# Split-weight offsets by kind of unit, regrouped low products, and two block boundaries taken one token tile at a time

## The chip, the cores and the metric

The kernel runs on one core of a Trainium2 chip. The metric is device microseconds (us) of one launch; lower is better. TensorE (PE) does the matrix products, its weight loads are listed as PEld, VectorE is DVE, ScalarE is ACT, GpSimd is POOL, and SP issues the weight stream.

## The reference, cut to what matters

Three transformer layers on x (256 tokens x 1024, fp32). Layer 1: differential attention beside a causal pool, cross-attention to a memory of 256 tokens, a SwiGLU of width 2816, each with a norm before and a norm after. Layer 2: retention beside sparse attention, then SwiGLU. Layer 3: HGRN2, then SwiGLU, then the final norm. What the change touches:

```python
x = x + rmsnorm(attn @ w_xo, g_x_post)          # "xo"
hf = rmsnorm(x, g_ffn_pre)
ff = (silu(hf @ w_gate) * (hf @ w_up)) @ w_down # "gu0", "dn0"
x = x + rmsnorm(ff, g_ffn_post)
proj = rmsnorm_2(x, norm_mix_g[0]) @ even_w_in  # "ev", first units: the queries
```

## The kernel before, in words

**Units.** All weights come as a stream of 165 units of 128 x 2048 fp32 (1 MB). SP loads unit u into `raw[:, u % 4]`; ACT writes its rounded high part to `whi` (`split`, L453); DVE writes the rest, raw minus high, to `wlo` (L937); PE uses both. PE waits for `lo_ready`, ACT for `unit_done` of the unit four back, SP for `lo_ready` of the unit four back. Activations are split as well: `x2[:, kt, :]` holds for block kt of 128 channels 256 columns of high parts (`xTh`) and then 256 of low parts (`xTl`); `hTh`/`hTl` hold the hidden layer.

**Kinds of unit.** Each product is high*high + high*low + low*high.
- *columns* (22 units on x, 4 on the memory): weights stationary, activations moving, 48 matmuls of 256 columns (`passes`, L1732 to L1734).
- *rows* (14 on x, 4 on the memory): activations stationary, weights moving, 48 of 256.
- *sums* ("out", "xo", "eo", "oo" and the three "dn"): activations stationary, weights moving, 24 of 512: four PSUM banks, two blocks, three passes (`sum_unit`). "xo" and "out" take `x2`, and so do half of "eo" and "oo"; the other halves take `nh` and `ah`; the 33 "dn" units take `hTh`/`hTl`.
- *gate/up* (66 units, `wide_columns`): per kt two matmuls of 512 columns (high weights on all of `x2[:, kt]`, L1770) and two of 256 (low weights on `xTh`, L1768, for kt 0 L1774).

**SBUF offsets.** From the widths of the allocations: `raw`, `whi` and `wlo` start alike modulo 512 bytes, and a ring slot is 8192 bytes; pads put `x2` 64 bytes further modulo 512, `hTh`/`hTl` 256 bytes further, `memTh`/`memTl` 32. While PE streams the moving operand of one matmul, the weights of the next are read. The table has the moving operand's address minus the weights' address, modulo 256 bytes, before and after the change (a slot becomes 8448 bytes, so modulo 512 the difference alternates with the slot's parity after it).

| kind of unit | before | after |
|---|---|---|
| columns on x / on the memory | 64 / 32 | 192 / 192 |
| rows on x / on the memory | 192 / 224 | 192 / 192 |
| gate/up, 512 columns / 256 columns | 64 / 64 | 0 / 192 |
| sums from x2 / nh / ah | 192 / 64 / 0 | 0 / 0 / 0 |
| sums from hTh | 0 | 0 (low weights of the first two "dn" units: 64) |

**Boundary "xo" to gate/up (n=3).** `sum_unit` finishes unit after unit; only the last unit completes the four banks, one after another (bank c is chunk c: tokens 0 to 127 are chunks 0 and 1). `post_norm` then goes per chunk: ACT squares (L522), DVE `gained` (L1023), mean, POOL power (L375), DVE `update` (L1030), which counts up `x_part`. PE's `boundary` transposes chunk 0, runs two dummy fp32 matmuls (`keep_clock`, L1821), then chunk 2, chunk 1, low products, chunk 3; ACT (`norm_hi`, L471) and DVE (`norm_lo`, L965) split the transposed blocks in eight steps of 256 columns. `first_wide` is unit gu0+0; behind it `rb_spread` (L1988) transposes the row scales, on which ACT waits (`rb_copy`) before it splits unit gu0+3, and DVE behind it:

```python
def norm(n, last, first):            # ACT
    ...
    split(last - 1 + RING)
    rb_copy(n)
    split(last + RING)
```

The boundary from "dn0" to "ev" (n=4) is the same with `first_columns`.

**Gate/up loop.** For each pair of units DVE does, in this order: reduce gate (L1072), times rb (L1082), `split` of unit +4, reduce up (L1072), times gate (L1091), `split` of unit +5, low part of h (L1096). ACT's silu (L537) waits on L1082, and its splits of units +4 and +5 stand behind the silu. Before the first "dn" unit PE also waits for `up_sum` of pair 9 (the first L1072 of `s_hb` behind the split of dn0+0).

Of the kernel before, what the change touches and what calls it, by code (L numbers as in the profile page):

```python
# [37 lines left out]
UNIT = 2048  # L38
RING = 4
# [36 lines left out]

POW_N = {"subln": 8, "gn0": 4, "gn1": 4, "hg0": 8, "hg1": 8}
# [27 lines left out]
N_GAIN = _at  # L105

# [13 lines left out]
def build(nc, stream, x_in, mem_in, pos_in, gains_in, rows_in, consts_in, poolm_in, wpool_in, retm_in,  # L120
# [12 lines left out]
    with ctx:  # L133

        raw = sb(ctx, "raw", [P, RING, UNIT])
        whi = sb(ctx, "whi", [P, RING, UNIT], F32R)
        wlo = sb(ctx, "wlo", [P, RING, UNIT], F32R)
# [6 lines left out]
        gains = sb(ctx, "gains", [P, N_GAIN])  # L144
# [14 lines left out]
        def gain(name, k=0):  # L159
# [8 lines left out]
        a_ = ExitStack()  # L168
        memTh = sb(a_, "memTh", [P, KT, S], F32R)
# [15 lines left out]
        posi = sb(a2, "posi", [P, S], I32)  # L185
        a2.close()
# [8 lines left out]
        sb(f_, "h_pad", [P, 56])  # L195
# [37 lines left out]
        sb(b4, "nh_pad", [P, 8])  # L233
# [9 lines left out]
        kd = sb(c_, "kd", [P, 8, S])  # L243
# [7 lines left out]
        sb(c_, "ah_pad", [P, 56])  # L251
        ah = sb(c_, "ah", [P, 4, S], F32R)
        al = sb(c_, "al", [P, 4, S], F32R)
        oh = qd[:].rearrange("p (g t a) (b n) -> p g t (a b) n", g=2, t=NT, n=P)
# [14 lines left out]
                 ("ffn1", "f1", 6)]  # L269

# [29 lines left out]
        def norm_banks(n):  # L300

            if n == 2:
                return [DB[2], DB[3], TB[0], TB[1]]
            ph = {3: "xo", 4: "dn0", 5: "eo", 6: "dn1", 7: "oo"}.get(n)
            return DB if ph is None else [b for k, b in banks.items() if k not in SUMS[ph]]
# [63 lines left out]
        def _(pool):  # L369
# [18 lines left out]
            pool.dma_start(gains[:, GAIN["lam"][0]:], gains_in[:, GAIN["lam"][0]:]).then_inc(sem("lam_in"), 16)  # L388
# [53 lines left out]
        def _(act):  # L442
            def split(u, i=None):
# [9 lines left out]
                nc.scalar.activation(whi[:, u % RING, 0:n], raw[:, u % RING, 0:n], ACT.Copy)\  # L453
                    .then_inc(hi_ready, 1)

            def norm_squares(n, src, scratch, version=None, parts=range(4)):

                for c in parts:
# [3 lines left out]
                    if n == 0 and c % 2 == 0:  # L462
                        act.wait_ge(sem(f"x_in{c // 2}"), 16)
                    nc.scalar.activation(scratch(c), chunk(src, c), ACT.Square, scale=D ** -0.5,
                                         accum_out=ss[:, 16 + c:17 + c]).then_inc(sem("norm_sq"), 1)

# [12 lines left out]
            def norm(n, last, first):  # L479
                norm_squares(n, xn, lambda c: chunk(y, c), NORMS[n][2], range(first))  # L480
                norm_hi(n, xTh)
# [32 lines left out]
            def post_squares(ph):  # L514

                for c in range(4):
                    wait_sum(act, ph, c)
# [38 lines left out]
            act.dma_start(gains[:, 0:GAIN["lam"][0]], gains_in[:, 0:GAIN["lam"][0]]).then_inc(sem("gains_in"), 16)  # L556
# [165 lines left out]
            post_squares("xo")  # L722
# [4 lines left out]
            post_squares("dn0")  # L727
# [192 lines left out]
        def _(dve):  # L920
# [8 lines left out]
            def split(u, i=None):  # L929

                if u >= N_UNITS:
# [5 lines left out]
                nc.vector.tensor_tensor(wlo[:, u % RING, 0:n], raw[:, u % RING, 0:n],  # L937
                                        whi[:, u % RING, 0:n], ALU.subtract).then_inc(lo_ready, 1)
# [20 lines left out]

            def norm_lo(n, dst_h, dst_l, kts=range(KT)):  # L960
# [14 lines left out]
            def norm_rest(n, last, between=None):  # L975

                name = NORMS[n][1]
                norm_lo(n, xTh, xTl)
# [8 lines left out]
            def evac_scaled(u, dst, src=None):  # L987
# [4 lines left out]
                    .then_inc(bank_read[bank(u)], 1)  # L992

# [16 lines left out]
            def post_norm(k0, ph, name):  # L1010
# [28 lines left out]
                gained(2)  # L1039
                update(1)  # L1040
# [127 lines left out]
            lam = gains[:, GAIN["lam"][0]:GAIN["lam"][0] + 256]  # L1168
# [154 lines left out]
            post_norm(1, "xo", "p_x")  # L1323
# [5 lines left out]
            post_norm(2, "dn0", "p_ffn")  # L1329
# [4 lines left out]
            def first_queries():  # L1334
                dve.wait_ge(sem("rb_ready"), 2)
                evac_scaled(u0, nqT[:, 0:2, :], DB[0])

            norm_rest(4, BASE["dn0"] + DN - 1, first_queries)
            evac_scaled(u0 + 1, nqT[:, 2:4, :])
# [388 lines left out]
        def _(pe):  # L1728
# [17 lines left out]
            def columns(u, act_h, act_l, ready=None):  # L1746

                hi = whi[:, u % RING, :].rearrange("p (k n) -> p k n", k=KT)
                lo = wlo[:, u % RING, :].rearrange("p (k n) -> p k n", k=KT)
# [10 lines left out]
            def wide_columns(u, o):  # L1760

                hi = whi[:, u % RING, :].rearrange("p (k n) -> p k n", k=KT)
                lo = wlo[:, u % RING, :].rearrange("p (k n) -> p k n", k=KT)
                c = [slice(P * f, P * f + P) for f in range(2)]
                for kt in range(KT):
                    if kt >= 1:
                        for f in range(2):
                            nc.tensor.matmul(o[:, f, 0:S], lo[:, kt, c[f]], xTh[:, kt, :], start=False, stop=False)  # L1768
                    for f in range(2):
                        ins = nc.tensor.matmul(o[:, f, :], hi[:, kt, c[f]], x2[:, kt, :], start=kt == 0,  # L1770
                                               stop=kt == KT - 1)
                    if kt == 0:
                        for f in range(2):
                            nc.tensor.matmul(o[:, f, 0:S], lo[:, kt, c[f]], xTh[:, kt, :], start=False, stop=False)  # L1774
                return ins

            def values_and_gates(u):

                n, c = 256 + NG_COLS, UNIT * (u % RING)
# [11 lines left out]
            def rows(u, act_h, act_l, ready=None, o=None, between=None):  # L1791

                hi = whi[:, u % RING, :].rearrange("p (k n) -> p k n", k=KT)
                lo = wlo[:, u % RING, :].rearrange("p (k n) -> p k n", k=KT)
# [23 lines left out]
            def keep_clock(bank_, times):  # L1818

                for _ in range(times):  # L1820
                    nc.tensor.matmul(bank_[:], ident, same_rows(cst[:, 0:256], 2), start=True, stop=True)  # L1821

# [11 lines left out]
            def first_unit():  # L1834

                hi, lo = (w[:, 0, :].rearrange("p (k n) -> p k n", k=KT) for w in (whi, wlo))
# [813 lines left out]
```

## Time and profile before

| | |
|---|---|
| median of 3 runs | 1045.02 us (1044.1 to 1045.32) |
| profiled execution | 1042.93 us, its span 1040.8 us |
| PE busy / weight loads | 1027.2 us (99%) / 914.5 us (88%) |
| DVE / ACT / POOL busy | 736.6 / 520.6 / 31.7 us |
| granted TensorE clock | 0.999 of 2.4 GHz |

Matmuls are pipelined, so a matmul's own duration (0.28 us for 256 columns, 0.39 for 512) says little; the time from one start to the next is what PE takes for it. "Busy 99%" means only that PE was rarely without work in flight.

### The profile page before, as it was taken

Reading aid. Unit: us, or ns where it says so; the run is one execution under the profiler, and the core shown is the slowest. Engines: PE = TensorE matmul, PEld = TensorE weight load, DVE = VectorE, ACT = ScalarE, POOL = GpSimd, SP = SyncE. Lnnn points to the kernel's source line nnn. Section 1 sums busy time; section 2 is a strip of 40 time slices with the busy share of each in tenths; the row PEclk is TensorE's granted clock in tenths of the full one; section 3 lists DMA queues with packets and bytes.
Section 4 is the critical chain, followed back from the end, with each engine's and each line's share of the span. In section 5 each row is a group of like instructions: output and inputs, shape, how many; then the busy total and the mean of one; then the engine's idle time right before and its main releaser. Section 6 shows DMA issues by size and latency. Waiting matters only on the chain.

```text
span 1040.8 us, 17117 instructions
## 1 busy us (share of the span) xinstructions
PE 1027.2 (99%) x6908; PEld 914.5 (88%) x6908; DVE 736.6 (71%) x946; ACT 520.6 (50%) x673; POOL 31.7 (3%) x49
## 2 busy tenths in 40 slices
PE   8999999999999999999999999999999999999997
PEld 7998898788888889999888888889999988888885
DVE  6987564568878545898768788646788767778842
ACT  6875474454344435865453443435543354443531
POOL 1000100000000001000000000001000100000000
PEclk9999999999999999999999999999999999999999
DMA  9834463255554746444235545655444235545531
GB/s 346 342 128 149 169 223 122 81 183 176 192 197 164 276 167 264 165 145 139 93 127 191 196 164 199 245 200 187 161 160 147 98 122 204 200 161 197 191 137 41
DMA packets 27292, 183.41 MB, mean 176 GB/s; under 512 B 3200, under 2 KB 3472, under 8 KB 6112
## 3 DMA queue, kind: packets, MB, share of 16 engines
q1 hardware_dynamic: 25056, 175.01, 47.2%
q0 software_dynamic: 1744, 7.16, 1.9%
q8 instruction: 46, 0.75, 0.3%
q10 hardware_dynamic: 432, 0.37, 0.1%
q14 instruction: 14, 0.11, 0.0%
HBM read 181.48 MB, written 1.05 MB: 175 GB/s over the span
## 4 chain that ended last, share of the span: by engine, by line
PE 94%; DVE 3%; ACT 2%; issue 1%; POOL 0%; DVEq 0%; ACTq 0%
PE GT L1770 12%; PE D L1770 11%; PE GT L1732 9%; PE GT L1734 9%; PE GT L1733 9%; PE D L1733 7%; PE D L1732 7%; PE D L1734 7%; PE GT L1768 5%; PE D L1768 5%; PE D L2443 1%; PE GT L1945 1%; DVE s_wlo L937 1%; PE GT L1774 1%; PE D L1774 1%
## 5 line engine op out<-in xcount | busy, mean ns | idle before, releaser
L937 DVE TENSOR_TENSOR s_wlo<-s_raw,s_whi 128x2048 fp32r<-128x2048 f32 x164 | 372.8, 2277 | 176.7 <-ACT s_whi L453 176.2
L453 ACT ACTIVATE s_whi<-s_raw 128x2048 fp32r<-128x2048 f32 x164 | 307.6, 1900 | 91.9 <-PE D L1734 68.7
L1770 PE MATMUL GT<-s_x,s_whi 128*128 128x512 f32 x528 | 162.1, 393 | 0.0
L1770 PE MATMUL D<-s_x,s_whi 128*128 128x512 f32 x480 | 146.9, 392 | 0.0
L1732 PE MATMUL D<-s_whi,s_hTh 128*128 128x512 f32 x264 | 102.9, 390 | 0.0
L1733 PE MATMUL D<-s_wlo,s_hTh 128*128 128x512 f32 x264 | 102.7, 389 | 0.0
L1734 PE MATMUL D<-s_whi,s_hTl 128*128 128x512 f32 x264 | 102.7, 389 | 0.0
L1732 PE MATMUL GT<-s_x,s_whi 128*128 128x256 f32 x352 | 99.6, 283 | 0.0
L1768 PEld LDWEIGHTS GT<-s_x,s_wlo 128*128 128x128 f32 x462 | 84.4, 188 | 16.9
L1734 PE MATMUL GT<-s_x,s_wlo 128*128 128x256 f32 x352 | 98.3, 279 | 0.0
L1733 PE MATMUL GT<-s_x,s_whi 128*128 128x256 f32 x352 | 98.2, 279 | 0.0
L1768 PE MATMUL GT<-s_x,s_wlo 128*128 128x256 f32 x462 | 91.4, 279 | 0.0
L1732 PE MATMUL GT<-s_whi,s_x 128*128 128x256 f32 (+2 forms) x296 | 90.9, 307 | 0.0
L1768 PEld LDWEIGHTS D<-s_x,s_wlo 128*128 128x128 f32 x420 | 76.8, 188 | 15.4
L1734 PE MATMUL GT<-s_whi,s_x 128*128 128x256 f32 (+2 forms) x296 | 89.0, 301 | 0.0
L1733 PE MATMUL GT<-s_wlo,s_x 128*128 128x256 f32 (+2 forms) x296 | 89.0, 301 | 0.0
L537 ACT ACTIVATE s_sg<-s_sg 128x512 f32<-128x512 f32 x33 | 20.9, 632 | 128.2 <-DVE s_sg L1082 128.2
L1770 PEld LDWEIGHTS GT<-s_x,s_whi 128*128 128x128 f32 x528 | 82.3, 188 | 2.5
L1768 PE MATMUL D<-s_x,s_wlo 128*128 128x256 f32 x420 | 83.1, 279 | 0.0
L1770 PEld LDWEIGHTS D<-s_x,s_whi 128*128 128x128 f32 x480 | 75.0, 188 | 2.5
L1732 PEld LDWEIGHTS GT<-s_x,s_whi 128*128 128x128 f32 x352 | 66.0, 187 | 0.3
L1733 PEld LDWEIGHTS GT<-s_x,s_whi 128*128 128x128 f32 x352 | 66.1, 188 | 0.0
(385 smaller groups left out, 1735.2 us busy)
## 6 DMA issues: line engine op xcount, KB each, us to landing
s_raw<-in_stream SPq DMA_DIRECT2D x164, 1024.0 KB, 4.8
s_gb<-in_rows POOLq DMA_DIRECT2D x4, 512.0 KB, 4.2
s_xn<-in_x SPq DMA_DIRECT2D x2, 512.0 KB, 4.3
s_raw<-in_stream SPq DMA_DIRECT2D x4, 256.0 KB, 6.6
s_y<-in_mem POOLq DMA_DIRECT2D x1, 1024.0 KB, 10.1
s_w<-in_cmpw POOLq DMA_DIRECT2D x1, 1024.0 KB, 11.5
s_poolm<-in_poolm POOLq DMA_DIRECT2D x1, 768.0 KB, 11.7
s_retd<-in_retm POOLq DMA_DIRECT2D x1, 768.0 KB, 7.1
```

What stands on the lines that cost most here:

```text
L453: nc.scalar.activation(whi[:, u % RING, 0:n], raw[:, u % RING, 0:n], ACT.Copy)\
L537: nc.scalar.activation(sg[:, q % 2, :], sg[:, q % 2, :], ACT.Silu).then_inc(sem("silu_made"), 1)
L937: nc.vector.tensor_tensor(wlo[:, u % RING, 0:n], raw[:, u % RING, 0:n], whi[:, u % RING, 0:n], ALU.subtract).then_inc(lo_ready, 1)
L1732: nc.tensor.matmul(out_, sh, mh, start=start, stop=False)
L1733: nc.tensor.matmul(out_, sh, ml, start=False, stop=False)
L1734: return nc.tensor.matmul(out_, sl, mh, start=False, stop=stop)
L1768: nc.tensor.matmul(o[:, f, 0:S], lo[:, kt, c[f]], xTh[:, kt, :], start=False, stop=False)
L1770: ins = nc.tensor.matmul(o[:, f, :], hi[:, kt, c[f]], x2[:, kt, :], start=kt == 0, stop=kt == KT - 1)
L1774: nc.tensor.matmul(o[:, f, 0:S], lo[:, kt, c[f]], xTh[:, kt, :], start=False, stop=False)
L1945: ins = nc.tensor.matmul(o[:, f, :], hi[:, kt, c], x2[:, kt, :], start=False, stop=kt == KT - 1)
L2443: ins = nc.tensor.matmul(DB[2 * hg + idx % 2][half * part:half * part + half, c:c + w], kd[:, h, tk], queries, start=True, stop=True)
```

## The change

1. `whi` and `wlo` slots get a pitch of 2112 elements, and `places(u)` shifts each unit's high and low part in its slot by 0, 16, 32 or 64 elements by its kind. Pads move `memTh`, `hTh`, `nh`, `ah` to match; `lam` gets its own tile; `ah` shares memory with `kd`.
2. `wide_columns` does all 16 low matmuls together, behind the first two high ones.
3. `last_sums`: the last two units of "xo" and "dn0" are summed bank by bank (12 matmuls each), and chunks 0 and 1 are transposed inside the fourth bank.
4. `first_pair` replaces `first_wide` of gu0 and `first_columns` of "ev": units 0 and 1 together, first the high weights on token tile 0, then the transposes of chunks 2 and 3, then tile 1 and all low products: 48 matmuls of 256 columns per unit. `tile_hi`/`tile_lo` split the transposed blocks in 8 steps of 128 columns for each tile. `rb_spread` follows the pair. `keep_clock` is gone.
5. `evac_wide` (a reduction and a product on DVE) takes the place of `evac_scaled` for ev+0 and ev+1.

```diff
+PITCH = UNIT + 64
+ROWS, SUM, COLUMNS, JOINED = 0, 16, 32, 64
+def places(u):
+    name = max((b, name) for name, b in BASE.items() if b <= u)[1]
+    j = u - BASE[name]
+    if name.startswith("gu") or name in ("ev", "dn0", "dn1", "dn2") and j < 2:
+        return SUM, COLUMNS
+    if name in SUMS or name == "out2":
+        return SUM, SUM
...
@@ ACT
+            def tile_hi(n, t):
+                for kt in range(KT):
+                    if kt % 4 == 0:
+                        if t == 0:
+                            act.wait_ge(sem("first_tr"), 2 * (n - 3) + kt // 4 + 1)
+                        else:
+                            act.wait_ge(sem("norm_tr"), 4 * n + kt // 2 + 2)
...
             def post_squares(ph, n=None):
                 for c in range(4):
+                    if n is not None and c == 3:
+                        tile_hi(n, 0)
@@ DVE post_norm
+                    update(1)
+                    gained(2)
+                    tile_lo(n, 0)
                 dve.wait_ge(sem("post_sq"), 4 * k0 + 4)
@@ PE wide_columns
+                for f in range(2):
+                    nc.tensor.matmul(o[:, f, :], hi[:, 0, c[f]], x2[:, 0, :], start=True, stop=False)
                 for kt in range(KT):
-                    if kt >= 1:
-                        for f in range(2):
-                            nc.tensor.matmul(o[:, f, 0:S], lo[:, kt, c[f]], xTh[:, kt, :], start=False, stop=False)
                     for f in range(2):
+                        nc.tensor.matmul(o[:, f, 0:S], lo[:, kt, c[f]], xTh[:, kt, :], start=False, stop=False)
+                for kt in range(1, KT):
+                    for f in range(2):
+                        ins = nc.tensor.matmul(o[:, f, :], hi[:, kt, c[f]], x2[:, kt, :], start=False,
@@ PE
+            def last_sums(ph, n, read, ready):
+                last = N_OF[ph] - 1
...
+                for b, o in enumerate(sum_banks(ph)):
...
+                    for j in (last - 1, last):
...
+                        for kk in range(2):
+                            if b == 3 and j < last and kk == 1:
+                                chunk_transposes(n, 0)
+                                chunk_transposes(n, 1)
...
+            def first_pair(n, u, pair):
...
+                for k, o in enumerate(pair):
+                    wait_unit(u + k)
+                    for kt in range(KT):
+                        pe.wait_ge(sem("first_tile_lo"), KT * (n - 3) + kt + 1)
+                        high_weights(u + k, o, 0, kt, start=kt == 0, stop=False)
+                chunk_transposes(n, 2)
+                chunk_transposes(n, 3)
+                for k, o in enumerate(pair):
+                    lo = low(u + k).rearrange("p (k n) -> p k n", k=KT)
+                    for kt in range(KT):
+                        pe.wait_ge(sem("xT_ready"), KT * n + kt + 1)
+                        high_weights(u + k, o, 1, kt, start=False, stop=False)
...
@@ PE mlp
+                        if i is None and q == 0 and f == 0:
+                            if c == 0:
+                                first_pair(n, u, gate_up_banks(0))
+                                rb_spread(n)
+                            continue
```

## Rows read from the trace of the kernel before

**Rows 1.** The page, parts 1 and 2: busy time, granted clock by slice.
```profile
PE 1027.2 (99%) x6908; PEld 914.5 (88%) x6908; DVE 736.6 (71%) x946; ACT 520.6 (50%) x673; POOL 31.7 (3%) x49
...
PEclk9999999999999999999999999999999999999999
```

**Rows 2.** Timeline, PE: "xo" and "dn0" sums. Start us, length us, instruction.
```profile
192.21 0.39 PE L1732 MATMUL GT<-s_whi,s_x 128*128 128x512 f32 x1
...
201.78 0.40 PE L1734 MATMUL D<-s_whi,s_x 128*128 128x512 f32 x1
...
378.94 0.39 PE L1732 MATMUL D<-s_whi,s_hTh 128*128 128x512 f32 x1
...
388.23 0.39 PE L1734 MATMUL D<-s_whi,s_hTl 128*128 128x512 f32 x1
```

**Rows 3.** Timeline, PE: gate/up units of gu0.
```profile
218.12 0.40 PE L1774 MATMUL D<-s_x,s_wlo 128*128 128x256 f32 x2
...
287.00 0.40 PE L1768 MATMUL D<-s_x,s_wlo 128*128 128x256 f32 x2
287.23 0.62 PE L1770 MATMUL D<-s_x,s_whi 128*128 128x512 f32 x2
...
323.49 0.40 PE L1774 MATMUL GT<-s_x,s_wlo 128*128 128x256 f32 x2
```

**Rows 4.** Timeline, PE: memory rows, slow and fast rows, columns on x.
```profile
91.36 0.28 PE L1733 MATMUL GT<-s_wlo,s_memTh 128*128 128x256 f32 x1
...
96.81 0.28 PE L1734 MATMUL GT<-s_whi,s_memTl 128*128 128x256 f32 x1
...
477.70 0.28 PE L1733 MATMUL GT<-s_wlo,s_x 128*128 128x256 f32 x1
...
483.12 0.28 PE L1734 MATMUL GT<-s_whi,s_x 128*128 128x256 f32 x1
...
717.86 0.28 PE L1733 MATMUL GT<-s_x,s_whi 128*128 128x256 f32 x1
...
727.17 0.28 PE L1734 MATMUL GT<-s_x,s_wlo 128*128 128x256 f32 x1
...
776.36 0.28 PE L1733 MATMUL GT<-s_wlo,s_x 128*128 128x256 f32 x1
...
781.58 0.28 PE L1734 MATMUL GT<-s_whi,s_x 128*128 128x256 f32 x1
```

**Rows 5.** Timeline, all engines: the boundaries behind "xo" and behind "dn0".
```profile
201.05 0.75 DVE L1030 SCALAR_TENSOR_TENSOR s_xn<-s_y,s_rstd,s_xn 128x512 f32<-128x512 f32 x1 [0.15 <-POOL s_rstd L375]
...
202.45 1.88 PE L1821 MATMUL GT<-s_cst 128*128 128x512 f32 x4
...
203.86 1.41 DVE L1030 SCALAR_TENSOR_TENSOR s_xn<-s_y,s_rstd,s_xn 128x512 f32<-128x512 f32 x2
...
206.80 1.57 ACT L471 ACTIVATE s_x<-GT,s_gains 128x256 fp32r<-128x256 f32 x4
...
207.68 1.66 DVE L965 SCALAR_TENSOR_TENSOR s_x<-GT,s_gains,s_x 128x256 fp32r<-128x256 f32 x4
...
211.87 0.38 PE L1988 MATMUL D<-s_cst,s_rstd 128*128 128x128 f32 x2
...
398.49 0.38 PE L1988 MATMUL D<-s_cst,s_rstd 128*128 128x128 f32 x2
```

**Rows 6.** Timeline, DVE and PE: the vector chain of gu0, its first and last pairs.
```profile
216.79 1.22 DVE L1072 TENSOR_REDUCE s_sg<-GT 128x512 f32<-128x1024 f32 x1
...
221.31 2.29 DVE L937 TENSOR_TENSOR s_wlo<-s_raw,s_whi 128x2048 fp32r<-128x2048 f32 x1 [2.50 <-ACT s_whi L453]
...
232.62 2.29 DVE L937 TENSOR_TENSOR s_wlo<-s_raw,s_whi 128x2048 fp32r<-128x2048 f32 x1 [2.50 <-ACT s_whi L453]
...
325.41 1.22 DVE L1072 TENSOR_REDUCE s_hb<-D 128x512 f32<-128x1024 f32 x1
...
328.59 0.39 PE L1732 MATMUL D<-s_whi,s_hTh 128*128 128x512 f32 x1
```

More of the change, by code:

```diff
@@ L74 @@
 LATE_KV = ("kv5", "out2", "kv6")
+ROWS, SUM, COLUMNS, JOINED = 0, 16, 32, 64
[6 more added lines that the diff above has]
+        return SUM, SUM
+    if name == "ev" and j == 4:
+        return JOINED, JOINED
+    columns = {"in": (4, 5, 6, 7), "kv": (0, 1, 2, 3), "xq": (0, 1, 2, 3), "ev": (0, 1, 2, 3, 6, 7, 8, 9),
+               "od": range(8)}
+    return (COLUMNS, COLUMNS) if j in columns.get(name, ()) else (ROWS, ROWS)
 POW_N = {"subln": 8, "gn0": 4, "gn1": 4, "hg0": 8, "hg1": 8}
@@ L105 @@
 N_GAIN = _at
+LAM = GAIN["lam"][0]
 def bank_reads(u):
@@ L269, in build, with high, low @@
                  ("ffn1", "f1", 6)]
+        def high(u, n=UNIT):
+            return whi[:, u % RING, places(u)[0]:places(u)[0] + n]
+        def low(u, n=UNIT):
+            return wlo[:, u % RING, places(u)[1]:places(u)[1] + n]
         def halves(ap):
@@ L452, in split @@
                 n = KT * NG_COLS if u == NG_UNIT else UNIT
-                nc.scalar.activation(whi[:, u % RING, 0:n], raw[:, u % RING, 0:n], ACT.Copy)\
+                nc.scalar.activation(high(u, n), raw[:, u % RING, 0:n], ACT.Copy)\
                     .then_inc(hi_ready, 1)
@@ L977, in norm_rest @@
                 name = NORMS[n][1]
-                norm_lo(n, xTh, xTl)
+                if n < 5:
+                    tile_lo(n, 1)
+                else:
+                    norm_lo(n, xTh, xTl)
                 norm_mean(n, name, 0)
@@ L1038, in post_norm @@
                 update(0)
-                gained(2)
-                update(1)
+                if n is None:
+                    gained(2)
+                    update(1)
+                else:
+                    update(1)
+                    gained(2)
+                    tile_lo(n, 0)
                 dve.wait_ge(sem("post_sq"), 4 * k0 + 4)
@@ L1834, in first_unit @@
             def first_unit():
-                hi, lo = (w[:, 0, :].rearrange("p (k n) -> p k n", k=KT) for w in (whi, wlo))
+                hi, lo = (w(0).rearrange("p (k n) -> p k n", k=KT) for w in (high, low))
                 def step(t, kt, stat, mov, start=False, stop=False):
@@ L1864, in second_unit @@
             def second_unit(u):
-                hi, lo = (w[:, u % RING, :].rearrange("p (k n) -> p k n", k=KT) for w in (whi, wlo))
+                hi, lo = (w(u).rearrange("p (k n) -> p k n", k=KT) for w in (high, low))
                 o = G[bank(u)]
@@ L1927, in first_wide, with part @@
             def first_wide(u, o, n):
-                def low(f):
+                def part(f):
                     return o[:, f, 0:S]
-                hi = whi[:, u % RING, :].rearrange("p (k n) -> p k n", k=KT)
-                boundary(n, u, low, 1)
+                hi = high(u).rearrange("p (k n) -> p k n", k=KT)
+                boundary(n, u, part, 1)
                 for kt in range(KT):
@@ L1937, in first_wide @@
                     if kt >= 4:
-                        block_low(u, low, n, kt, 1)
+                        block_low(u, part, n, kt, 1)
                     for f in range(2):
@@ L1970, in first_queries @@
                 u, n = BASE["xq"], 2
-                hi, lo = (w[:, u % RING, :].rearrange("p (k n) -> p k n", k=KT) for w in (whi, wlo))
+                hi, lo = (w(u).rearrange("p (k n) -> p k n", k=KT) for w in (high, low))
                 wait_unit(u)
@@ L2052, in mlp @@
                 pe.wait_ge(sem("up_sum"), p0 + GU // 2 - 1)
-                for d in range(DN):
+                for d in range(DN - 2 if f == 0 else DN):
                     pe.wait_ge(sem("h_lo"), p0 + d + 1)
                     sum_unit(f"dn{f}", d, hTh, hTl, n=6 if f == 1 and d == DN - 1 else None)
+                if f == 0:
+                    last_sums("dn0", 4, "h_lo", p0)
             pe.wait_ge(sem("warm_in"), 1)
@@ L2237, in _ @@
             x_out(3)
-            for j in range(1, 4):
-                pe.wait_ge(sem("x_lo"), j + 1)
-                sum_unit("xo", j)
+            pe.wait_ge(sem("x_lo"), 2)
+            sum_unit("xo", 1)
+            last_sums("xo", 3, "x_lo", 0)
             mlp(0)
@@ L2264, in ret_out @@
                     .then_inc(sem("ret_out"), 1)
-            first_columns(u0, 4)
+            first_pair(4, u0, (DD[:, 0:2, :], GT[:, 2:4, :]))
             rb_spread(4)
-            for j in range(1, 4):
+            for j in range(2, 4):
                 unit(u0 + j, columns)
```

142 lines of the change are left out of this document (95 added, 47 removed).

## The prediction

> **What bounds the kernel now.** The page comes first. PE is busy 99% of the span at a granted clock of 0.999, which is its upper level of 2.4 GHz, and DVE 71% [rows 1]. So the time is that of PE's matmuls one after another, and a change can only shorten it by making PE start them closer together, by taking out waits of PE, or lengthen it by making PE wait. The second view is PE's timeline, read from start to start. In "xo" 42 matmuls of 512 columns start over 9.57 us, 233.4 ns each; in "dn0" 42 of the same form over 9.29 us, 226.6 ns each [rows 2]. Clock, size and pattern are the same; what differs is the difference of the two operands' addresses (192 against 0 in the table of offsets). A gate/up unit takes (323.49 - 218.12) / 19 = 5.546 us; a pair of its low products takes 0.23 us, so that each of the 16 of 512 columns takes about 230 ns [rows 3]. Units of 256-column matmuls have two paces. Columns on x: 9.31 us over 79 steps, 117.8 ns (21 of the 22 units). Rows on x: 5.22 / 46 = 113.5 ns in ten units, 5.42 / 46 = 117.8 in four, with the same offsets. Memory rows: 118.5 [rows 4]. The third view is the timeline of all engines at the two boundaries, where PE waits for the post norm; the fourth is DVE's in gate/up, which shows how far the supply of low parts is ahead of PE.
>
> **Offsets.** I take the address difference as the cause of the paces, since it is what the two groups of [rows 2] do not share.
> - Sums from x2, without xo+2 and xo+3: 240 matmuls x 6.8 ns = -1.6 us. For those from nh and ah I take nothing; the bound is -0.6.
> - Gate/up, 512 columns: difference 0, so 226.6. Its 256-column ones get the difference of the row units on x, whose mean is (10 x 113.5 + 4 x 117.8) / 14 = 114.7. A unit: 16 x 226.6 + 16 x 114.7 = 5.461 us, 0.085 less. 42 units of gu1 and gu2: -3.6 us. Regrouping the low products adds nothing: the counts are the same, and low behind low and low behind high take alike.
> - Columns on x, without ev+1: 21 x 48 = 1008 matmuls, 117.8 to 114.7, -3.1 us. Bounds: -4.3 (all fast) and 0 (all slow).
> - Memory, 384 matmuls at 118.5 or 117.8: -1.3 us, between -1.8 and 0.
> - The low weights of two units in each "dn" have difference 64: 48 matmuls at 230 for 226.6, +0.15 us.
>
> The Trainium skill, TensorE: Matmul & The Clock Gate, section "Step-by-step: what each phase is for", speaks against all of this: PE reads moving operand and weights through two independent ports, and loading the next weights takes no bandwidth from the running matmul. By that rule offsets are worth nothing. The 233.4 beside 226.6 does not agree with it; it is the fourth rival below.
>
> **Boundary behind "dn0".** Before, from the start of the second-last unit: 48 x 226.6 = 10.88 us to 388.46, then 10.03 to the row scales at 398.49 [rows 5], 0.2 for them, and ev+1 in 48 x 117.8 = 5.65: 26.8 us until ev+2 can start. After: 10.88; eight transposes inside it, 0.88 (four took 202.01 to 202.45); 32 high matmuls on tile 0 at 115 ns, 3.68; eight transposes, 0.88; a wait; 64 matmuls, 7.36; 0.2.
>
> Are tile 0's parts there in time? Count from the end of bank 1. Before, that was 12 matmuls ahead of the end of bank 3 at 202.01, or 199.21, and the first `update` began 1.84 us behind it, at 201.05, the second follows 0.7 later, so chunk 1 is ready at 3.5; PE reaches its transposes at 2.72 + 0.68 + 0.44 = 3.84. ACT takes 1.57 for four blocks of 256 columns and DVE 1.66 [rows 5]. A block of 128 costs half to all of that; I take two thirds, 0.26, nearer to half because the fixed part of an instruction stays. Then tile 0 is split by 7.6, and PE, which gets there at 6.3, takes 0.23 per kt and stays behind the supply. Bank 3's square, mean, power and updates end near 9.9; PE wants chunks 2 and 3 at 10.0 and 10.4. All that hides. What does not: tile 1's first four highs, then its first low, behind the transposes of chunk 2: 0.2 + 4 x 0.27 + 0.1 + 0.4 - 0.44 (chunk 3) = 1.4 us of wait, where before 2.2 us went to waiting and dummy matmuls (202.45 to 204.67). Bounds of the wait: 0.9 and 2.0. After: 10.88 + 0.88 + 3.68 + 0.88 + 1.4 + 7.36 + 0.2 = 25.3. That is -1.5 us. `evac_wide` (a reduction of 1.2 us and a product) comes between DVE's splits of ev+2 and ev+3, which have 5.5 us of PE work as cover: nothing, and up to 2 us if the cover failed.
>
> **Boundary behind "xo" and all of gu0.** The same step costs here, because it moves `rb_spread` behind two units. ACT's `rb_copy` and its split of gu0+3 wait for it, DVE's split of gu0+3 waits for ACT, and behind that stands the first gate reduction, with which the chain of the phase starts. Call the time of the row scales F. Before F is 211.87, the first reduction starts at 216.79, and the low part of gu0+4 is done at 221.31 + 2.29 = 223.60 = F + 11.7. The chain's period is 232.62 - 221.31 = 11.31 us, longer than PE's pair of 11.09, and it was ahead because PE still had gu0+1 to do behind F. Now PE has only gu0+2 and gu0+3: it wants gu0+4 at F + 0.2 + 2 x 5.46 = F + 11.1. So it waits 0.6 us, and then 11.31 - 10.92 = 0.4 us in each pair: gu0 runs at DVE's pace, whatever its offsets give. The "dn" start waits for `up_sum` of pair 9, at 326.63 = F + 114.8 [rows 6], and dn0+2 starts 10.9 later. From the start of xo+2 (190.81) to dn0+2 (328.59 + 10.88 = 339.47), before: 148.7 us. After: 10.88 (now at 226.6) + 0.88 + 3.68 + 0.88 + 1.4 + 7.36 + 125.7 = 150.8. +2.1 us. In gu1 and gu2 nothing is moved; PE gets there 21 x 0.085 = 1.8 us earlier and the margin is 328.59 - 326.63 = 1.96, so they just escape, and a larger gain than 2 us in either would be lost.
>
> **Sum.** -1.6 - 3.6 - 3.1 - 1.3 + 0.15 - 1.5 + 2.1 = -8.9 us. Of the units in the attention phases some end in front of a wait for another engine, which takes back part; I allow 0.4. -8.5 us against the profiled execution's 1042.9 gives 1034.4 us. That execution is 2.1 us below the median of the runs, so for the median 1045.0 - 8.5 = **1036.5 us**.
>
> **Rivals.**
> 1. *DVE's chain does not bind gu0.* It would have to be ahead at F by 5.3 us more than I reckon; for it speaks only that my F rests on the boundary's reckoned wait. gu0 then gives 20 units at 5.461: 145.4 for 150.8, 1031 us.
> 2. *The 256-column matmuls stay at 117.8.* For it: the row units show both paces at the same offsets, and one column unit was fast at the old ones, so the offset is not all. Then columns and memory give 0.1, gate/up 16 x 3.4 - 16 x 0.8 = 0.04 per unit, 1.7 us, and the rest stays: about -2.5, 1042.5 us.
> 3. *Slower.* No 512-column matmul of the kernel before has a difference of 0 modulo 512 bytes: "dn0" stands at 256 or 768. The new slot pitch gives half of the units 0. If those run at 226.6 + x, the price is (396 of "dn" + 192 of other sums + 336 of gu1 and gu2) = 924 matmuls times x. Against it: the slowest pace seen is 233.4. From x = 9 ns (236) the gain is gone, from 11.5 (238) the kernel is slower by over 0.2%; at 240 it takes about 1049 us.
> 4. *Offsets do nothing.* Then only the boundaries count: +2.5 and -1.3, 1046.2 us.
>
> **How the numbers follow.** The forecast 0.5, with 1034 to 1039 as its own range; rival 1 0.14; rival 2 0.17; rival 3 0.07; rival 4 0.07; something else 0.05. The range from rival 1 to rival 2 and its edge, 1031 to 1043, leaves out rivals 3 and 4 and part of the rest. A measurement of this kernel tells about 0.2% (2.1 us) from no change. Faster by more than that: the forecast, rival 1, two thirds of rival 2, part of the rest, 0.79. Within it: the remainder of rival 2, rival 4 and the mild form of 3, 0.12. Slower 0.09.
>
> **What the profile after would show.** "xo" and "out" sums at 226.6 ns per start; gate/up units of gu1 at 5.46 us; column units below 117.8; slots of both parities alike (rival 3 if not). At the boundaries one PE wait near 1.4 us, on DVE's first low part of tile 1, and no L1821. In gu0 a PE wait of 0.4 us on DVE's low part in every second unit, a period of 11.3 us per pair, and none in gu1 and gu2. The prediction is wrong if gu0 shows no such waits, or if the paces do not follow the table of offsets.

## The result, and the profile after

The changed kernel takes 1045.43 us in the median of 20 runs (1042.56 to 1047.22), the kernel before 1043.44 beside it (20 runs, 1042.68 to 1045.56): a ratio of 1.0016, 95% interval 1.0009 to 1.0022. It is slower by about 1.7 us (the medians differ by 2.0), where 8.5 us less were forecast. The profiled execution took 1046.54 us, 3.6 more than that of before; it is the third slowest of its 20 runs.

The page of the changed kernel, parts 1 and 4, and its waits of PE from 214 to 500 us (two views, the second from 340; us in total, times, longest):

```profile
span 1044.4 us, 17188 instructions
...
PE 1025.2 (98%) x6930; PEld 915.7 (88%) x6930; DVE 741.3 (71%) x964; ACT 523.7 (50%) x689; POOL 31.5 (3%) x49
...
PE 80%; DVE 8%; ACT 6%; issue 6%; DVEq 0%; ACTq 0%
...
PE D L1814 <- DVE s_hb L1155: 1.2, 1, 1.2
PE GT L1848 <- DVE s_wlo L991: 0.4, 1, 0.4
...
PE GT L1814 <- DVE s_nqT L1070: 2.6, 1, 2.6
PE D L2015 <- DVE s_x L1024: 1.2, 1, 1.2
```

PE's busy time did fall by 2.0 us against [rows 1], but the chain of work that ended last now runs through DVE and ACT for 14% of the span. On the page of the kernel before that line reads:

```profile
PE 94%; DVE 3%; ACT 2%; issue 1%; POOL 0%; DVEq 0%; ACTq 0%
```

That is a share of the chain and not time lost: most of it is DVE's chain in gu0, which PE now follows. The largest single wait of PE, 2.6 us for the evacuation of ev+0, is not in the prediction's sum.

PE's timeline after, at the points that answer to [rows 2 to 6] (start, length, instruction, idle before it):

```profile
189.35 0.39 PE L1814 MATMUL GT<-s_whi,s_x 128*128 128x512 f32 x1
...
207.19 0.51 PE L2015 MATMUL GT<-s_x,s_whi 128*128 128x256 f32 x2 [1.18 <-DVE s_x L1024]
...
226.72 0.72 PE L1848 MATMUL GT<-s_x,s_whi 128*128 128x512 f32 x2 [0.39 <-DVE s_wlo L991]
...
237.97 0.73 PE L1848 MATMUL D<-s_x,s_whi 128*128 128x512 f32 x2
...
249.37 0.72 PE L1848 MATMUL GT<-s_x,s_whi 128*128 128x512 f32 x2
...
329.74 0.47 PE L1814 MATMUL D<-s_whi,s_hTh 128*128 128x512 f32 x1 [1.20 <-DVE s_hb L1155]
...
340.96 0.39 PE L1814 MATMUL D<-s_whi,s_hTh 128*128 128x512 f32 x1
...
379.06 0.39 PE L1814 MATMUL D<-s_whi,s_hTh 128*128 128x512 f32 x1
...
407.49 0.36 PE L1814 MATMUL GT<-s_x,s_whi 128*128 128x256 f32 x1 [2.55 <-DVE s_nqT L1070]
...
549.11 0.61 PE L1848 MATMUL D<-s_x,s_whi 128*128 128x512 f32 x2
549.56 2.05 PE L1851 MATMUL D<-s_x,s_wlo 128*128 128x256 f32 x16
551.45 3.36 PE L1854 MATMUL D<-s_x,s_whi 128*128 128x512 f32 x14
554.65 0.61 PE L1848 MATMUL GT<-s_x,s_whi 128*128 128x512 f32 x2
...
727.78 0.28 PE L1814 MATMUL GT<-s_x,s_whi 128*128 128x256 f32 x1
...
733.22 0.28 PE L1814 MATMUL GT<-s_x,s_whi 128*128 128x256 f32 x1
```

In gu0 the units at 226.72, 237.97 and 249.37 are every second one. They start 11.25 and 11.40 us apart, where two units without a wait take 11.08: PE waits a little in each pair, mostly too briefly to be listed as a wait. A gate/up unit outside gu0 takes 554.65 - 549.11 = 5.54 us, as before (5.546): its 16 low products start 118 ns apart (551.45 - 549.56), and its 14 high ones behind them take 3.20 us, 228.6 each. The column unit from 727.78 takes 5.44 us over 48 starts, 113.3. And the windows view, which shows what the wait at 407.49 brought with it (columns: PE busy, granted clock, DMA share, GB/s):

```profile
404.40:407.40 3.00, 0.54 (x5) 1.00 1.03 407
407.40:411.60 4.20, 4.11 (x22) 0.60 0.99 392
411.60:438.00 26.40, 25.96 (x272) 1.00 0.65 241
438.00:442.50 4.50, 4.50 (x38) 0.62 0.49 204
```

Behind the wait the granted clock is at its lower level, 1.2 GHz, for 3.3 us (from 408.2 to 411.5 it is 0.51), and it is there again for some 3 us from 439. A column matmul then starts 213 ns behind the last one and not 113 to 118; 16 and 14 such starts make 1.5 and 1.4 us. Before, the clock was 1.00 all the way from 390 to 440.

Every run has a mean granted clock on record, and the time goes with it. Of the changed kernel's 20 runs 13 are at 0.996 or less; of the 81 runs of the kernel before beside the experiments one is. The four runs of the changed kernel at 0.998 have a mean of 1043.7 us (1042.56 to 1045.37), the seven at 0.995 one of 1046.1; the 48 of before at 0.998 have 1043.0. So most of the loss in the median comes with the lower clock. This compares few runs, on chips that are partly not the same, and is not an experiment.

Where the 3.6 us of the two profiled executions come from, by PE's starts (ends of the stretches as in [rows 2 to 5] and above):

| stretch | before | after | difference |
|---|---|---|---|
| to the start of xo+2's sums | 190.81 | 189.35 | -1.5 |
| xo+2 to dn0+2 (boundary, gu0) | 148.7 | 151.6 | +2.9 |
| second-last dn0 unit to ev+2 | 26.8 | 28.4 | +1.6 |
| ev+2 to the first "eo" sum (both half-clock stretches) | 96.9 | 99.9 | +3.0 |
| the rest | | | -2.4 |

### The profile page after: what moved, and what is told of

Read it like the earlier page. It is cut to its first block, busy times and chain, and to the rows that moved or that the text cites. A ratio compares the mean times of both kernels' runs of the same rounds, so it can differ in the third digit from the quotient of the medians.

```text
span 1044.4 us, 17188 instructions
## 1 busy us (share of the span) xinstructions
PE 1025.2 (98%) x6930; PEld 915.7 (88%) x6930; DVE 741.3 (71%) x964; ACT 523.7 (50%) x689; POOL 31.5 (3%) x49
## 4 chain that ended last, share of the span: by engine, by line
PE 80%; DVE 8%; ACT 6%; issue 6%; DVEq 0%; ACTq 0%
PE GT L1814 8%; PE GT L1815 8%; PE GT L1816 8%; PE D L1814 7%; PE D L1816 7%; PE D L1815 7%; PE GT L1854 7%; PE D L1854 6%; PE GT L1851 4%; PE D L1851 4%; ACT s_whi L489 3%; DVE s_wlo L991 2%; PE D L2577 1%; DVE s_hb L1155 1%; PE GT L2015 1%
## 5 line engine op out<-in xcount | busy, mean ns | idle before, releaser
L1854 PE MATMUL GT<-s_x,s_whi 128*128 128x512 f32 x448 | 107.6, 391 | 0.0
L1854 PE MATMUL D<-s_x,s_whi 128*128 128x512 f32 x420 | 100.9, 391 | 0.0
L1814 PE MATMUL GT<-s_x,s_whi 128*128 128x256 f32 x336 | 96.4, 287 | 2.6 <-DVE s_nqT L1070 2.6
L1854 PEld LDWEIGHTS GT<-s_x,s_whi 128*128 128x128 f32 x448 | 82.0, 188 | 15.7
L1815 PE MATMUL GT<-s_x,s_whi 128*128 128x256 f32 x336 | 94.9, 283 | 0.0
L1816 PE MATMUL GT<-s_x,s_wlo 128*128 128x256 f32 x336 | 94.9, 282 | 0.0
L1814 PEld LDWEIGHTS GT<-s_x,s_whi 128*128 128x128 f32 x336 | 64.8, 193 | 3.0 <-issue 2.8
L1851 PEld LDWEIGHTS GT<-s_x,s_wlo 128*128 128x128 f32 x512 | 64.7, 189 | 2.5
L1851 PE MATMUL GT<-s_x,s_wlo 128*128 128x256 f32 x512 | 65.4, 281 | 0.0
L1816 PEld LDWEIGHTS GT<-s_x,s_wlo 128*128 128x128 f32 x336 | 64.8, 193 | 0.0
L1815 PEld LDWEIGHTS GT<-s_x,s_whi 128*128 128x128 f32 x336 | 64.7, 193 | 0.0
L1851 PEld LDWEIGHTS D<-s_x,s_wlo 128*128 128x128 f32 x480 | 60.6, 189 | 2.3
```

Of the source, the lines that this page charges most:

```text
L1814: nc.tensor.matmul(out_, sh, mh, start=start, stop=False)
L1815: nc.tensor.matmul(out_, sh, ml, start=False, stop=False)
L1816: return nc.tensor.matmul(out_, sl, mh, start=False, stop=stop)
```

## The experiments

All ratios are against the kernel before on the same chip, with 95% intervals.

**The parts by themselves.** Three kernels divide the change: its offsets alone, its boundaries alone, and offsets with the grouped low products.

```diff
 # e1: offsets; old boundaries, old order        # e2: old offsets and order; new boundaries
-PITCH = UNIT                                    -    first_wide(...); first_columns(u0, 4)
+PITCH = UNIT + 64                               +    last_sums(...); first_pair(...)
+... high(u), low(u) with places(u)              # e5: e1 and the low products of gate/up together
```

> The changed kernel's offsets and pads, with the order of the kernel before: its post-norm boundaries and its low products between the high ones in gate/up. Theory A (the offsets pay, the new boundaries lose it): sums from x2 near 227 to 229 ns, the two first units of each dn near 232, no wait in gu0; about 3 us below the kernel before, 1040.5. Rival B (the offsets do nothing or cost): within 1 us of the kernel before, 1043.4.

> The changed kernel's boundaries (chunkwise last sums, first pair tile by tile) on the layout, offsets and gate/up order of the kernel before. Theory A: 2.6 us lost from the end of xo to dn0, 1.6 us at the boundary behind dn0, and 1.6 to 2.9 us more because PE's granted clock falls behind its wait there: 1048.5 to 1050. Rival B (the loss belongs to the offsets): within 2 us of the kernel before.

> The changed kernel with both post-norm boundaries of the kernel before: offsets and low products together, nothing else. Theory A (in gate/up the new offsets alone cost 0.054 us per unit, 5.600 for 5.546, and taking the low products together gives 0.060): 63 units times 0.060 below the kernel with the offsets alone, 1044.2 - 3.8 = 1040.4 us, units of 5.54. Rival B (the units keep 5.60 without the boundaries' order around them): 1044.

| kernel | us | ratio |
|---|---|---|
| e1, offsets | 1044.18 | 1.0012 (1.0003 to 1.0021) |
| e2, boundaries | 1048.54 | 1.0050 (1.0038 to 1.0063) |
| e5, offsets and grouping | 1040.68 | 0.9968 (0.9955 to 0.9981) |

The boundaries alone cost 0.5%; offsets and grouping together gain 0.32%. The boundaries came out as expected of e2, and e5 as its theory A. But e1 missed its expectation: offsets alone, with the old interleaved order, gain nothing (rival B). PE's timeline of e1, the first low product (kt 0) of two gate/up units in a row:

```profile
543.25 0.40 PE L1858 MATMUL D<-s_x,s_wlo 128*128 128x256 f32 x2
...
548.85 0.40 PE L1858 MATMUL GT<-s_x,s_wlo 128*128 128x256 f32 x2
```

5.60 us, where [rows 3] give 5.546: the new offsets cost gate/up 0.054 us a unit (512 columns start 233.8 ns apart), 3.4 us over the 63 units that are not the first of their phase. That eats the gain of the sums. The grouping gives 0.06 back: 63 x 0.06 = 3.8, as measured between e1 and e5 (3.5 us, or 4.6 by the ratios).

**Is it the grouping or the offset that helps gate/up?**

```diff
 # e6: offsets of before, grouped     # e7: e5, but in places(u):
-PITCH = UNIT + 64                    -        return SUM, COLUMNS   # gu*, and dn0 to dn2, ev with j < 2
+PITCH = UNIT                         +        return SUM, SUM
```

> The layout and offsets of the kernel before, its boundaries, and only the low products of gate/up together. Theory A (a run of 512-column matmuls goes at 226.6 only at a difference of 0; at 64 it goes at some 232, as the first two units of each dn do): a gate/up unit of 16 x 117.8 + 14 x 232 + 2 x 227 = 5.59 us, 1043.0 + 63 x 0.04 = 1045.5. Rival B (grouping alone sets the unit, offsets do nothing in gate/up): units of 5.54, 1042.6.

> As the kernel with the old boundaries, the new offsets and the low products together, but the low parts of gate/up, of the first two units of each dn and of ev+0 and ev+1 at offset 16 instead of 32. The first two units of each dn then have difference 0: 227 instead of 232 ns per matmul, 6 units x 0.13 = 0.8 us less. For the 256-column matmuls of gate/up: theory A (their pace does not follow the difference) units stay at 5.54, 1039.6 in all; rival B (a difference of 192 is what lets 256 columns go fast) they slow down beyond 117.8; at 119 to 121 it is 63 x 16 x 1.2 to 3.2 ns more, 1040.8 to 1042.8.

e6: 1041.12 us, 0.9977 (0.9967 to 0.9986); e7: 1041.05 us, 0.9978 (0.9967 to 0.9988). PE's timeline of e6, then of e7, from gate/up unit to unit:

```profile
535.85 0.62 PE L1844 MATMUL D<-s_x,s_whi 128*128 128x512 f32 x2
536.31 1.98 PE L1847 MATMUL D<-s_x,s_wlo 128*128 128x256 f32 x16
...
541.32 0.62 PE L1844 MATMUL D<-s_x,s_whi 128*128 128x512 f32 x2
541.78 2.05 PE L1847 MATMUL D<-s_x,s_wlo 128*128 128x256 f32 x16
...
546.88 0.39 PE L1844 MATMUL GT<-s_x,s_whi 128*128 128x512 f32 x1
```

```profile
538.07 0.62 PE L1850 MATMUL D<-s_x,s_whi 128*128 128x512 f32 x2
538.52 2.08 PE L1853 MATMUL D<-s_x,s_wlo 128*128 128x256 f32 x16
...
543.63 0.39 PE L1850 MATMUL D<-s_x,s_whi 128*128 128x512 f32 x1
```

In e6 units take 5.47 and 5.56 us in turn, 5.52 in the mean. Both theories of e6 were wrong: at a difference of 64 the grouped unit is not slower but faster than with the change's offsets (5.54), because every second run of 256-column products goes at 113.3. Its 512-column ones start 229 ns apart in the mean, not 232 as theory A had it. In e7, where the 256-column products stand at a difference of 0, they take 119.6 ns each and a unit 5.56 us; rival B was right for the pace. The first two units of each "dn" went from some 232 to 226.7, as reckoned. The medians of e5, e6 and e7 lie within 0.4 us and do not tell these layouts apart; the starts do. So grouping pays at either layout, and in gate/up the change's offsets take part of it back.

**The wait at ev+2.** ev+0 and ev+1 now stand in D and in banks 2 and 3 of GT; ev+2 and ev+3 write banks 0 and 1 of GT. They waited all the same, since `wait_bank` counts units and not banks. e3 leaves the two units out of the count, e8 does so with the old boundary behind "xo", which is also tried by itself (e4). e4 and e8 have the dummy matmuls behind "xo" again, but not behind "dn0".

```diff
 # e3 and e8
             n = bank_reads(u)[bank(u)]
+            if u in (BASE["ev"] + 2, BASE["ev"] + 3):
+                n -= 1
 # e4 and e8: sum_unit("xo", j) for j in 1..3, first_wide and keep_clock behind "xo"
```

> The changed kernel, but ev+2 and ev+3 no longer count the evacuations of ev+0 and ev+1, whose banks are others. Theory A (that wait of 2.55 us, and the half clock of 3.3 us behind it, are the loss at this boundary): no wait at ev+2, granted clock 1.0 there, 3 to 4 us below the changed kernel, about 1041.5 to 1042.5. Rival B (DVE's chain is only uncovered one step later): ev+3 or ev+4 waits 1 to 2.5 us instead, and less than 1.5 us is gained.

> The changed kernel with the old boundary behind xo (whole units, first unit alone, dummy matmuls), and the new one behind dn0. Theory A (the new step behind xo moves the row scales behind two units and makes gu0 run at DVE's pace): no waits in gu0, dn0 starts 2.6 us earlier against the end of xo, about 1043. Rival B (gu0's waits only take up what the boundary had gained): within 0.5 us of the changed kernel.

> The old boundary behind xo, the new one behind dn0, and ev+2 and ev+3 not counting the evacuations of ev+0 and ev+1. Theory A (the two losses add): what the bank wait cost in the profile, 2.6 us of wait and up to 1.6 of half clock, off the 1042.15 of the kernel with the old boundary behind xo: 1038.5 to 1040.5. Rival B (the new boundary behind dn0 brings a stretch of half clock somewhere in ev anyway, or DVE is late at ev+3): 1041 to 1042.

| kernel | us | ratio |
|---|---|---|
| e3, no bank wait | 1044.08 | 1.0011 (1.0002 to 1.0020) |
| e4, old boundary behind "xo" | 1042.15 | 0.9991 (0.9981 to 1.0002) |
| e8, both | 1040.22 | 0.9965 (0.9953 to 0.9978) |

First the changed kernel at this place, PE, ACT and DVE; then e3:

```profile
404.56 0.38 PE L2115 MATMUL D<-s_cst,s_rstd 128*128 128x128 f32 x2
...
404.98 0.38 ACT L526 ACTIVATE s_rb<-D 128x256 f32<-128x256 f32 x1 [4.47 <-PE D L2115]
...
405.39 1.22 DVE L1069 TENSOR_REDUCE s_nqT<-D 128x512 f32<-128x1024 f32 x1 [2.56 <-ACT s_rb L526]
406.65 0.69 DVE L1070 TENSOR_TENSOR s_nqT<-s_nqT,s_rb 128x512 f32<-128x512 f32 x1
```

```profile
378.46 0.39 PE L1814 MATMUL D<-s_whi,s_hTh 128*128 128x512 f32 x1
...
404.09 0.36 PE L1814 MATMUL GT<-s_x,s_whi 128*128 128x256 f32 x1
...
424.80 0.36 PE L1814 MATMUL GT<-s_x,s_whi 128*128 128x256 f32 x1 [0.99 <-ACT s_vsw L809]
```

and e3 by windows (PE busy, granted clock, DMA share, GB/s):

```profile
421.00:424.80 3.80, 2.81 (x72) 1.00 0.64 203
424.80:428.40 3.60, 3.60 (x18) 0.54 0.87 282
```

Row scales, copy, reduction and product, 2.8 us in a row, used to lie behind ev+1; with both units done at once nothing lies over them. In e3 ev+2 starts at once and the boundary takes 404.09 - 378.46 = 25.6 us (25.3 predicted, 26.8 before). In its profiled execution that is 3.9 us of span less (1040.5 for 1044.4): the wait, and one of the two stretches at half clock. Its median fell by only 1.35 us, and its interval overlaps that of the changed kernel (0.5 us by the ratios), so the medians do not show the gain. The profiled executions exaggerate it: e3's (1042.72) is the fastest of its 11 runs, the changed kernel's is among its slowest. One wait is new in e3: PE gets to ev+6 earlier and waits 0.99 us there for ACT to read out the values of ev+4, and the clock falls at that point. In e8 the same step took 1.9 us off e4's median, 2.7 by the ratios, and e8's granted clock is 1.00 from 400 to 450. Theory A holds for the wait, and rival B for part of its worth in e3; e8 is inside its own theory A.

e4 shows the other boundary by itself: PE waits nowhere from 204 to 345 us, and from the start of xo+2 to that of dn0+0 it takes 137.47 us, where the changed kernel takes 140.39 and the kernel before 137.78. Its theory A holds.

**The waits in gu0.** Two different cures for DVE's chain, each with both new boundaries and without the bank wait: in e9 the next high split comes ahead of the silu, in e10 the split of gu0+3 comes ahead of the copy of the row scales.

```diff
 # e9, ACT, pair(q)                              # e10, ACT, norm(3)
+    split(u0 + 2 * q + RING, i)                      split(last - 1 + RING)
     act.wait_ge(sem("gate_sum"), ...)           -    rb_copy(n)
     nc.scalar.activation(... ACT.Silu)               split(last + RING)
-    split(u0 + 2 * q + RING, i)                 +    rb_copy(n)
```

> Both new boundaries, ev+2 and ev+3 without the bank wait, and in gate/up ScalarE splits the next gate unit ahead of the silu instead of behind it. In the trace of the changed kernel VectorE waits 2.50 us in each pair for that split. Theory A (the chain reduction, gain, silu, high split, low split sets the period of 11.3 us, and nothing else does): the period falls to PE's 11.08, PE waits in gu0 only for the first pair or not at all, 2.6 us less than the 1044.1 without this: 1041.5. Rival B (VectorE's own work binds): the waits of 0.3 us per pair stay and the time is 1044.

> Both new boundaries, ev+2 and ev+3 without the bank wait, and behind xo ScalarE splits gu0+3 ahead of the copy of the row scales instead of behind it. Theory A (gu0's waits come from the late start of the chain, because that split stands behind the row scales): the first gate reduction starts some 4 us earlier against the first unit's end, PE waits nowhere in gu0, 2.6 us less: 1041.5. Rival B (the chain is slower than PE and the waits return within gu0): less than 1.5 us less.

e9: 1039.76 us, 0.9969 (0.9958 to 0.9980); e10: 1040.52 us, 0.9965 (0.9954 to 0.9976); 4.3 and 3.6 us below e3 (4.4 and 4.8 by the ratios), where theory A had 2.6. DVE in the changed kernel, in e9 and in e10:

```profile
219.78 1.22 DVE L1155 TENSOR_REDUCE s_sg<-GT 128x512 f32<-128x1024 f32 x1
...
224.30 2.29 DVE L991 TENSOR_TENSOR s_wlo<-s_raw,s_whi 128x2048 fp32r<-128x2048 f32 x1 [2.50 <-ACT s_whi L489]
...
235.62 2.29 DVE L991 TENSOR_TENSOR s_wlo<-s_raw,s_whi 128x2048 fp32r<-128x2048 f32 x1 [2.51 <-ACT s_whi L489]
```

```profile
221.56 2.28 DVE L991 TENSOR_TENSOR s_wlo<-s_raw,s_whi 128x2048 fp32r<-128x2048 f32 x1
...
230.28 2.28 DVE L991 TENSOR_TENSOR s_wlo<-s_raw,s_whi 128x2048 fp32r<-128x2048 f32 x1
```

```profile
211.10 4.49 DVE L994 TENSOR_TENSOR s_wlo<-s_raw,s_whi 128x2048 fp32r<-128x2048 f32 x2 [1.65 <-ACT s_whi L489]
...
215.58 1.22 DVE L1158 TENSOR_REDUCE s_sg<-GT 128x512 f32<-128x1024 f32 x1
```

The period of the changed kernel's chain is 235.62 - 224.30 = 11.32 us, and 2.5 of it is DVE waiting for an ACT split that stood behind the silu for no reason of data. Without that (e9) the first steps take 8.72 each (221.56 to 230.28), until DVE has caught up with PE near 257; from there DVE waits for PE. In e10 the period stays at 11.3, but the first gate reduction starts 4.2 us earlier (215.58 for 219.78), and PE does not catch up with the chain within the phase. In both PE waits nowhere from 214 to 345 us, and from xo+2 to dn0+0 they take 136.55 and 136.54 us for 140.38 in e3: 3.8 us less. So the chain cost more than the 2.6 that theory A took: its unlisted waits in each pair add up to 2.2 us beside the listed 0.39 and 1.20. Without them the new boundary behind "xo" is 0.9 us shorter than the old one (137.47 in e4). Here the prediction's account of gu0 is shown, from two sides.

**Offsets once more, on the better kernel.** e11 is e8 on the old layout, e12 is e8 with gate/up at the old difference of 64 (the same line puts the first two units of each "dn" at 192), e14 is e12 with all column units at 64 too, those on the memory included, and e13 is everything that helped: both boundaries, no bank wait, e9's order, gate/up at 64.

```diff
 # e12 and e13, places(u)                        # e14, places(u), besides
-        return SUM, COLUMNS   # gu*, ...        -    return (COLUMNS, COLUMNS) if j in columns... else (ROWS, ROWS)
+        return ROWS, ROWS                       +    return ROWS, ROWS
```

> The old boundary behind xo, the new one behind dn0 without the bank wait, the low products of gate/up together, on the layout and offsets of the kernel before. With the new offsets this took 1040.2. Theory A (the offsets give 1.6 us in the sums and 1.5 in the columns of od, and take 1.2 in gate/up and 0.8 in dn): 1 us more, 1041.3. Rival B (the offsets give nothing in all): 1039.5 to 1040.5.

> As the fastest kernel so far (1040.2: old boundary behind xo, new one behind dn0 without the bank wait, new offsets), but gate/up, the first two units of each dn, ev+0 and ev+1 at offset 0, where their difference is the old one of 64. Theory A (gate/up goes by its own difference: 5.520 us per unit at 64, as on the old layout, for 5.540): 63 x 0.02 = 1.3 us less, with 48 more matmuls per dn at 232, which takes 0.5 back: 1039.5. Rival B (the layout does not matter, the old alternation of 5.483 and 5.557 came from the banks or the slots): 1040.2 or, with dn's part, 1041.

> As the kernel with the old boundary behind xo, the new one behind dn0 without the bank wait and gate/up at offset 0 (1039.3), but the column units at offset 0 too, so that their difference is the old 64 instead of 192. Theory A (192 lets a column unit run at 113.3, 64 holds it at 117.8): od+1 to od+7 and xq+3 at 117.8, 1.6 us more, 1040.9. Rival B (the pace is set by what went before, not by the difference): od+1 to od+7 stay at 113.3 to 113.7, 1039.3.

> Both new boundaries, ev+2 and ev+3 without the bank wait, the split ahead of the silu, and gate/up at offset 0 (difference 64). Theory A (what the runs gave adds up): the 1039.3 of the kernel with the old boundary behind xo, less the 0.7 us that the new one is shorter once gu0 does not wait: 1038.6. Rival B (the boundary behind xo gives nothing): 1039.3 or more.

| kernel | us | ratio |
|---|---|---|
| e11, old layout | 1041.92 | 0.9981 (0.9972 to 0.9990) |
| e12, gate/up at 64 | 1039.30 | 0.9960 (0.9946 to 0.9973) |
| e14, columns at 64 as well | 1041.76 | 0.9984 (0.9975 to 0.9993) |
| e13, all that helped | 1037.46 | 0.9949 (0.9935 to 0.9963) |

PE's starts of od+2 and od+3, in e14 and then in e10, whose column units stand at 192:

```profile
722.61 0.28 PE L1816 MATMUL GT<-s_x,s_whi 128*128 128x256 f32 x1
...
728.26 0.28 PE L1816 MATMUL GT<-s_x,s_whi 128*128 128x256 f32 x1
```

```profile
723.32 0.28 PE L1817 MATMUL GT<-s_x,s_whi 128*128 128x256 f32 x1
...
728.97 0.28 PE L1817 MATMUL GT<-s_x,s_whi 128*128 128x256 f32 x1
```

Both units take 5.65 us, 117.8 per start. At 64 all of od+1 to od+7 go so, in e14 and in the four other kernels with that difference (before, e2, e6, e11). At 192 they go at 113.3 to 113.7 in ten kernels, and only in e10 did od+1 to od+4 stay at 117.8, with the same addresses. Theory A of e14 and of e11 holds for this stretch. It is no rule for the whole kernel: e6 ran two of the four column units of "in", and ev+1 to ev+3, at 113.3 with a difference of 64. e14 lost 2.5 us against e12, more than the 1.6 of its theory; in the traces two column units on the memory and three of "ev" go at 117.8 for 113.3 as well, 1.1 us more. The difference shifts which pace a unit falls into; it does not fix it.

e12's units of gate/up alternate like e6's, 5.52 in the mean: the alternation belongs to the difference, not to the layout. In the median e12 is 0.9 us below e8, which the intervals do not show to be a gain. e13 spends 336.83 - 189.62 = 147.2 us from xo+2 to dn0+2 (148.6 with the old boundary in e4), and its granted clock is 1.00 in every window from 400 to 450 us. It beats both kernels: it is 5.9 us below the one before. That is 1.1 below what the sum of the parts gave, which five runs do not tell from nothing.

## Why the prediction was wrong, step by step

- **Sums from x2** (-1.6): right. They went from 233.0 to 233.5 down to 226.6 to 228.8; over the ten units outside the boundary that is 1.3 us. Rival 3 is out: from dn0+3 on the units take 226.7 in slots of either parity. The Trainium skill, TensorE: Matmul & The Clock Gate, section "Step-by-step: what each phase is for", has the two operands come through independent ports, by which nothing could change; the trace does not agree with it. Rival 4 is out as a mechanism. Its number, 1046.2, is nearer to the result than any other of the prediction's, and that is chance: the offsets moved the paces both ways (e1), and their gains and costs nearly cancel.
- **Gate/up** (-3.6, the largest term): the first of two steps that failed. It took the paces of two uniform runs (226.6, 114.7) for a unit that changes between them, and said that regrouping adds nothing. It measured -0.3: the low products went at 117.8, and the first five high ones behind them took 234, 236, 228, 232 and 231 before 226.6 was reached. Without the grouping the offsets would have cost 3.4 (e1), and at the old offsets the grouping alone gives 0.026 us per unit (e6). The 256-column part is rival 2.
- **Columns** (-3.1, bounds -4.3 and 0): "od" gave 1.4 and the others some 0.6, inside the bounds. The difference matters (e14), but does not decide alone (e10, e6).
- **Memory** (-1.3): about -0.6.
- **First units of "dn"** (+0.15): +0.8. I had charged the low third of the matmuls. All three passes slowed to some 232, and the unit behind them still takes 227.7. So a third of the matmuls at another difference slows the others too. e7 takes it away; at 192 for all of them (e12) these units take 233.3.
- **Boundary behind "dn0"** (-1.5): +1.6, and 1.5 more at half clock. This is the second step that failed. The PE work between the sums and the row scales was reckoned well (25.3; 25.6 in e3). The error is a sentence of the prediction: "`evac_wide` comes between DVE's splits of ev+2 and ev+3, which have 5.5 us of PE work as cover: nothing". I had asked who waits for DVE's splits and not who waits for the evacuation itself. ev+2's bank wait counted it, and its cover, ev+1, had moved in front of the row scales. The 2 us named for a failed cover were near the 2.55 measured, but they had no rival and no place in the range.
- **Boundary behind "xo" and gu0** (+2.1): +2.9, the mechanism as told: 1.18 us at the boundary (1.4 reckoned), 0.39 at gu0+4 and 1.20 at dn0+0, and a chain period of 11.32 us (11.31). e9 and e10 show it, so rival 1 is out. The first dn0 matmul came 114.9 us behind the row scales (114.8 reckoned). Freed of the chain, the new boundary would have gained 0.9 us.
- **The clock** was in no term: it was put at nothing without a reason, though the change takes out the dummy matmuls that were there for it. Two stretches at 1.2 GHz cost some 1.5 and 1.4 us in the profiled execution. No kernel has the new boundary behind "dn0" with dummy matmuls, so what leaving them out cost is open.

Of the 12.1 us between 3.6 lost in the profiled executions and 8.5 forecast, gate/up is 3.3 us, the boundary behind "dn0" 3.1, the clock 2.9, and the rest is from the smaller terms. Not settled: why the 256-column matmuls keep one of two paces for a whole unit, and what makes the clock fall in one execution and not in another. The mean clocks on record say only that it falls more in the changed kernel than in the one before.

## What to carry to other kernels

When an edit completes two units at once instead of one after the other, list every semaphore that the next unit waits for, including those that count by position where the memory is no longer shared: the unit that moved was the cover of each of them. A pace measured in a uniform run does not carry over to a mixed one; measure the mixed unit. And look in a chain for what one engine does in front of the work that others wait for: once the new boundary had uncovered that chain, moving a split ahead of the silu, one line, was worth more than the offsets.

## What the runs showed of the hardware

- **Address difference.** 512-column matmuls start 226.6 ns apart at a difference of 0 modulo 256 bytes ("dn", and the sums from x2 after the change), 233.3 at 192 (the same sums before, the first "dn" units in e12 to e14) and 229 in the mean at 64, in a cycle of 226, 229 and 232 (gate/up in e6 and e12). Where a third of them stand at 64 and the rest at 0, all take 232 in the mean. 256-column ones take 119.6 at 0 (gate/up in e7), and at 64 and at 192 either 117.8 or 113.3, one pace for a whole unit. In the changed kernel five 512-column ones pass behind a run of 256 columns before the pace is 226.6.
- **Granted clock.** It fell to half for some 3 us within 1.5 us behind the start that ended a wait of 2.55 us, in each of the three kernels with that wait (the changed kernel, e2, e4) and in none without it. It also fell around the stretch of small matmuls between ev+5 and ev+7, with waits of a microsecond or less: from 425 in e3, and from 434 in e5, which has the old boundary and its dummy matmuls. e5 by windows (PE busy, granted clock, DMA share, GB/s):

```profile
421.00:434.90 13.90, 13.47 (x176) 0.98 0.79 288
434.90:437.60 2.70, 2.70 (x15) 0.50 0.19 79
```

  In one execution of each kernel it fell there in two of the five with dummy matmuls behind "dn0" (e5 and e7; not in the kernel before, e1 and e6) and in nine of the eleven without (not in e8 and e13). So the dummies do not rule the fall out, and whether they make it rarer is open. A window that lies inside a fall reads 0.50 or 0.51, any other 1.00, and those between straddle an edge. The two levels agree with the Trainium skill, TensorE: Matmul & The Clock Gate, section "Part 1: The HAM clock gate", which knows a full and a half rate. The section also says that the moment of the change differs from run to run; with one trace of each kernel no run here shows that.
